# Attention of a hybrid encoder block in couples of steps instead of single steps, with the PSUM banks laid out anew

## The chip, the cores and the metric

The kernel runs on one core of one Trainium2 chip. The metric is the device time of one execution in microseconds (us); lower is better. Five engines work side by side on a core: TensorE (PE), VectorE (DVE), ScalarE (ACT), GpSimd (POOL) and SyncE (SP, which only issues DMAs here). They are kept in order by semaphores alone.

## What is computed

One layer of an encoder on 1024 tokens of width 1024, all in f32. The part that the change touches is attention over a token's own chunk of 64 and the 8 chunks before it, for 8 heads of width 64:

```
u = layer_norm(x) * (1 + sc_m) + sh_m
z_q, z_k, z_v, z_gate = pieces of u @ w_in
s = einsum('bnqhd,bnkhd->bnhqk', q, kb) + bias      # q scaled by 64 ** -0.5
p = softmax(s, axis=-1)                             # over 9 chunks, those ahead of the start left out
o = einsum('bnhqk,bnkhd->bnqhd', p, vb)
merged = gate0 * y_pool + gate1 * (o @ w_br_attn) + gate2 * y_conv
```

Around it stand adaLN conditioning, a pooling branch, a convolution branch, an output projection and an MLP. Each product is made of three fp32r products (high by high, high by low, low by high), which keeps nearly f32 accuracy; so each operand is split into a rounded part and its rest.

## The kernel before, in words

The program writes out by hand, engine by engine, in which order each instruction stands; nothing schedules it. The heads are taken in 4 pairs, each pair in 16 steps: `step_of` (L433) makes of a step number a pair, a head h of the two, and a block t of 128 queries out of 8. There are 64 steps. A step of block t has min(t+1, 5) key blocks of 128, so t = 0 to 3 are narrow and t = 4 to 7 wide (5 blocks, 640 keys).

What one step goes through:

- **scores** (PE, L2387): 2 matmuls where the keys fit one bank, else 4 (320 columns each).
- **add_scores** (DVE, L1683): the bias is added, the row's maximum taken and the result negated, in one instruction that writes `probs`, and a short one that reads the maximum out. It signals `biased`.
- **the exponential** (ACT, L1123), with the row's sum; then the sum's reciprocal (DVE, L1718); then the scaling of `probs` (ACT, a `copy`, L938). They signal `exp_done`, `inv_done` and `probs_done`.
- **transpose_probs** (PE, L2397): one 128x128 transpose per key block, into PSUM.
- **take_pt_hi** (ACT, L938) rounds the transposed weights into `pt`, **take_pt_lo** (DVE, L1701) makes the rest. `pt` has two places, for even and odd steps.
- **weigh** (PE, L2412): one matmul of 256 columns per key block, values by weights, into PSUM (`o_bank`).
- **take_low** (ACT, L938) copies one part of the result to `mid`; **add_o** (DVE, L1693 and L1695) adds the two others, one after the other, each of 64 partitions by 128 columns. It signals `o_added`, two counts a step.

The queries, keys and values of the next pair are projected meanwhile: 144 matmuls of 512 columns a pair (`project`, L2347), nine a step. In the pair's first two steps PE also transposes the values (`transpose_v`, L2368; `take_v`, `take_v_lo` take them off). `take_half` on ACT and `take_half_lo` on DVE take the projections off; `cut_hi_after` and `cut_lo_after` split the next weights.

On PE step a stands as: scores of a, five projections, transposes of a-1, four projections, weighing of a-2. On DVE (the loop after L1703): add_scores of a, what there is to take of a projection, the reciprocal of a, add_o of a-3, take_pt_lo of a-1. PSUM's eight banks of 512 f32 columns: 0 and 1 projections, 2 and 3 weighed values of even and odd steps, 4 and 5 scores (5 also transposed values), 6 and 7 transposed weights.

Of the kernel before, what the change touches and what calls it, by code (L numbers as in the profile page):

```python
# [7 lines left out]
P = 128  # L8
# [48 lines left out]
PER_STEP = PROJ // STEPS  # L57
# [16 lines left out]
def trunk_layer(nc, x, c, w_ada, b_ada, w_in, b_gate, w_pool, pool_scale, rel_bias, conv_w, conv_b,  # L74
# [180 lines left out]
    with ExitStack() as ctx:  # L255
# [189 lines left out]
        def score_cols(t):  # L445

            if width_of(t) <= HALF:
                return ps[:, 4, 0:width_of(t)]
            return ps[:, 4:6, 0:KEYS // 2]
# [16 lines left out]
        def o_bank(b, rows, part):  # L466
            return ps[rows, 2 + b % 2, part * P:(part + 1) * P]
# [291 lines left out]
        def _(pool):  # L759
# [151 lines left out]
            for t in range(4, ST - 1):  # L911
# [3 lines left out]
        HALF_STEP = {2: (0, 0), 3: (0, 1), 5: (1, 0), 6: (1, 1), 8: (2, 0), 9: (2, 1), 10: (3, 0), 11: (3, 1),  # L915
                     13: (4, 0), 15: (5, 0)}
        CUT_STEP = {7: 1, 12: 3, STEPS + 1: 5}

        def half_of(a):

            pair, i = divmod(a, STEPS)
            if 0 <= pair < PAIRS and i in HALF_STEP and not (pair == PAIRS - 1 and i in (3, 6, 9, 11)):
                return pair + 1, *HALF_STEP[i]
            return None

        def cut_of(a):

            for pair in range(PAIRS):
                if a - STEPS * pair in CUT_STEP:
                    return pair + 1, CUT_STEP[a - STEPS * pair]  # L930
            return None

        N_STEPS = PAIRS * STEPS

        @block.scalar
        def _(act):
# [137 lines left out]
            def take_v(pair, half):  # L1074
# [7 lines left out]
                if pair >= 2:  # L1082
                    act.wait_ge(pv_done, STEPS * (pair - 1))
                copy(v_high(pair % 2, slice(4 * half, 4 * half + 4)),
                     ps[:, 5, :].rearrange("p (t c d) -> p t c d", t=4, d=HEAD_DIM)).then_inc(vt_hi, 1)
# [21 lines left out]
            def take_pt_hi(b):  # L1107

                nb = blocks_of(step_of(b)[2])
                act.wait_ge(pt_done, b + 1)  # L1110
                if b >= 2:
                    act.wait_ge(pv_done, b - 1)
                copy(pt[:, b % 2, 0:nb, 0, :], banks(6)[:, 0:nb * P].rearrange("p (b q) -> p b q", q=P))\
                    .then_inc(pt_hi_done, 1)

            for a in range(N_STEPS + 3):
                pair, h, t = step_of(a)
                if a >= 3:
                    take_low(a - 3)
                if a < N_STEPS:  # L1120
                    col, w = a % STAT_COLS, width_of(t)
                    act.wait_ge(biased, a + 1)
                    nc.scalar.activation(probs[a % 2][:, 0:w], probs[a % 2][:, 0:w], ACT.Exp,  # L1123
                                         bias=neg_max[:, col:col + 1], scale=-1.0,
                                         accum_out=row_sum[:, col:col + 1]).then_inc(exp_done, 1)
                if 1 <= a <= N_STEPS:
                    take_pt_hi(a - 1)
# [1584 lines left out]
```

## Time and profile before

| what | us |
|---|---|
| median of 3 runs (1402.46 to 1402.83) | 1402.79 |
| the profiled execution, its own time | 1402.69 |
| its span (first to last instruction) | 1400.9 |
| PE busy in the span | 1380.7 (99%) |
| DVE, ACT, POOL busy | 982.4, 652.7, 429.3 |
| attention steps, from the first scores to the last weighing | about 139 to 372 |

The span is what the trace covers; the execution's own time is 1.8 us longer. Busy time of PE counts the overlapping matmuls once. A row of the timeline gives the start in us from the span's start, the duration in us, the engine and the line, what is written and read, and how many like instructions stand together; behind it, in brackets, idle time of the engine before it and what ended that. PEld is the load of the stationary operand, which runs beside the matmul before.

### The profile page before, as it was taken

Reading aid. Unit: us, or ns where it says so; the run is one execution under the profiler, and the core shown is the slowest. Engines: PE = TensorE matmul, PEld = TensorE weight load, DVE = VectorE, ACT = ScalarE, POOL = GpSimd, SP = SyncE. Lnnn points to the kernel's source line nnn. Section 1 sums busy time; section 2 is a strip of 40 time slices with the busy share of each in tenths; the row PEclk is TensorE's granted clock in tenths of the full one; section 3 lists DMA queues with packets and bytes.
Section 4 is the critical chain, followed back from the end, with each engine's and each line's share of the span. In section 5 each row is a group of like instructions: output and inputs, shape, how many; then the busy total and the mean of one; then the engine's idle time right before and its main releaser. Section 6 shows DMA issues by size and latency. Waiting matters only on the chain.

```text
span 1400.9 us, 17410 instructions
## 1 busy us (share of the span) xinstructions
PE 1380.7 (99%) x6560; PEld 1151.1 (82%) x6560; DVE 982.4 (70%) x1356; ACT 652.7 (47%) x925; POOL 429.3 (31%) x454
## 2 busy tenths in 40 slices
PE   6999999999999999999999999999999999999997
PEld 4888888888888888888888888888888888888886
DVE  7899777776499935564588797655656736447688
ACT  7523777877522133112436754444334635343251
POOL 1023655656565000000035236334344200001225
PEclk9999999999999999999999999999999999999999
DMA  9985466474665234653702645443446978466371
GB/s 344 330 277 151 137 188 172 155 198 152 205 193 173 91 105 131 219 161 120 262 8 114 217 144 195 158 156 131 150 158 224 310 265 286 171 224 239 102 228 77
DMA packets 159083, 256.42 MB, mean 183 GB/s; under 512 B 11352, under 2 KB 81422, under 8 KB 159000
## 3 DMA queue, kind: packets, MB, share of 16 engines
q1 hardware_dynamic: 144152, 204.97, 44.0%
q0 software_dynamic: 14848, 50.34, 10.8%
q8 instruction: 52, 0.85, 0.3%
q14 instruction: 31, 0.25, 0.1%
HBM read 182.36 MB, written 68.71 MB: 179 GB/s over the span
## 4 chain that ended last, share of the span: by engine, by line
PE 90%; DVE 5%; ACT 2%; SPq 1%; issue 1%; DMA 1%; DVEq 0%; ACTq 0%
PE ps L2181 23%; PE ps L2182 23%; PE ps L2183 23%; PE ps L2347 12%; PE ps L2387 2%; PE ps L2412 2%; PE ps L2397 2%; DVE bn L1426 1%; DVE mid L1877 1%; DMA ada<-in_w_ada_dram 1%; PE ps L2288 1%; PE ps L2282 1%; PE ps L2283 1%; DVE mix_tmp L1870 1%; ACT mix_tmp L961 1%
## 5 line engine op out<-in xcount | busy, mean ns | idle before, releaser
L2001 DVE TENSOR_TENSOR part_lo<-k_raw,part_hi 128x1024 fp32r<-128x1024 f32 x112 | 147.1, 1343 | 56.8 <-ACT part_hi L938 53.8
L2182 PE MATMUL ps<-part_lo,part_hi 128*128 128x512 f32 (+1 forms) x460 | 176.4, 383 | 0.0
L2183 PE MATMUL ps<-part_hi,part_lo 128*128 128x512 f32 (+1 forms) x460 | 176.4, 383 | 0.0
L2181 PE MATMUL ps<-part_hi 128*128 128x512 f32 (+1 forms) x460 | 176.4, 383 | 0.0
L2181 PE MATMUL ps<-act_hi,w_hi 128*128 128x512 f32 (+1 forms) x448 | 171.6, 383 | 0.0
L2183 PE MATMUL ps<-act_hi,w_lo 128*128 128x512 f32 (+1 forms) x448 | 170.9, 382 | 0.0
L2182 PE MATMUL ps<-act_lo,w_hi 128*128 128x512 f32 (+1 forms) x448 | 170.9, 382 | 0.0
L938 ACT ACTIVATE part_hi<-k_raw 128x1024 fp32r<-128x1024 f32 x112 | 116.4, 1059 | 111.8 <-DMA k_raw<-tw_scratch 50.2
L1420 DVE TENSOR_TENSOR w_lo<-w_raw,w_hi 128x1024 fp32r<-128x1024 f32 x51 | 67.3, 1320 | 54.6 <-ACT w_hi L938 54.6
L2181 PEld LDWEIGHTS ps<-part_hi 128*128 128x128 f32 x460 | 86.4, 188 | 17.2
L2183 PEld LDWEIGHTS ps<-part_hi,part_lo 128*128 128x128 f32 x460 | 86.4, 188 | 17.0
L2182 PEld LDWEIGHTS ps<-part_lo,part_hi 128*128 128x128 f32 x460 | 86.4, 188 | 16.9
L1343 ACT ACTIVATE h_buf<-h_buf,cols 128x1024 f32<-128x1024 f32 x28 | 32.3, 1152 | 145.6 <-DVE h_buf L1996 145.6
L2347 PE MATMUL ps<-act_hi,w_lo 128*128 128x512 f32 x240 | 99.8, 416 | 0.0
L2183 PEld LDWEIGHTS ps<-act_hi,w_lo 128*128 128x128 f32 x448 | 84.2, 188 | 16.4
L2181 PEld LDWEIGHTS ps<-act_hi,w_hi 128*128 128x128 f32 x448 | 84.2, 188 | 16.3 <-issue 0.2
L2182 PEld LDWEIGHTS ps<-act_lo,w_hi 128*128 128x128 f32 x448 | 84.3, 188 | 16.1 <-issue 0.2
L2347 PE MATMUL ps<-act_hi,w_hi 128*128 128x512 f32 x240 | 94.8, 395 | 0.0
L2347 PE MATMUL ps<-act_lo,w_hi 128*128 128x512 f32 x240 | 94.3, 393 | 0.0
L938 ACT ACTIVATE w_hi<-w_raw 128x1024 fp32r<-128x1024 f32 x52 | 54.8, 1053 | 80.1 <-PE ps L2183 74.6
L897 POOL TENSOR_TENSOR resid<-resid,q 128x512 f32<-128x512 f32 x16 | 25.3, 1609 | 218.1 <-DVE q L2062 218.1
L2181 PE MATMUL ps<-act_hi,set_hi 128*128 128x512 f32 x224 | 87.1, 389 | 0.0
(294 smaller groups left out, 3279.2 us busy)
## 6 DMA issues: line engine op xcount, KB each, us to landing
k_raw<-h_scratch SPq DMA_DIRECT2D x112, 256.0 KB, 4.5
w_raw<-in_w_in_dram SPq DMA_DIRECT2D x41, 512.0 KB, 4.1
ada<-in_w_ada_dram SPq DMA_DIRECT2D x8, 2048.0 KB, 10.9
tw_rows<-in_w_ff_dram POOLq DMA_DIRECT2D x64, 256.0 KB, 4.1
tw_scratch<-tw_sum POOLq DMA_DIRECT2D x32, 512.0 KB, 3.5
h_scratch<-h_sum POOLq DMA_DIRECT2D x64, 256.0 KB, 2.9
k_raw<-tw_scratch SPq DMA_DIRECT2D x64, 256.0 KB, 5.4
pair_raw<-in_w_ff_dram SPq DMA_DIRECT2D x13, 1024.0 KB, 6.3
```

The source lines that it names most:

```text
L897: nc.gpsimd.tensor_tensor(row, row, quad[:, t % 4, :], ALU.add).then_inc(quad_added, 1)
L938: return nc.scalar.activation(out, in_, ACT.Copy, **kw)
L1343: nc.scalar.activation(row, row, ACT.Relu, bias=cols[:, R_FF1 + n:R_FF1 + n + 1]).then_inc(relu_done, 1)
L1420: nc.vector.tensor_tensor(lo[:, :, :], raw_part(n)[:, :, :], f(hi[:, :, :]), ALU.subtract)\
L2001: nc.vector.tensor_tensor(part_lo[s][:, :, :], k_raw[rs][:, :, :], f(part_hi[s][:, :, :]), ALU.subtract)\
L2181: nc.tensor.matmul(out, sh, mh, start=first, stop=False)
L2182: nc.tensor.matmul(out, sh, ml, start=False, stop=False)
L2183: return nc.tensor.matmul(out, sl, mh, start=False, stop=last)
L2347: ins = nc.tensor.matmul(ps[:, hz % 2, :], s, v, start=kk == 0, stop=kk == 23)
L2387: ins = nc.tensor.matmul(ps[:, 4 + part, 0:n], qs[s][:, h, t * P:(t + 1) * P], kd[s][:, term, h, ks], start=term == 0, stop=term == 1)
L2397: ins = nc.tensor.transpose(banks(6)[:, cs], probs[b % 2][:, cs], ident[:, :])
L2412: ins = nc.tensor.matmul(ps[:, 2 + b % 2, 0:2 * P], vs[s][:, t + 1 - nb + m, h * P:(h + 1) * P], pt[:, b % 2, m, :, :], start=m == 0, stop ...
```

## The change

The loop over steps becomes a loop over couples of steps: COUPLES = 32, PER_PAIR = 8. Couple u holds the steps a = 2u and a+1. On PE it stands as: both weighings of couple u-2, both groups of transposes of couple u-1, scores of a, six projections, scores of a+1, twelve projections. At the first couple of a pair (i = 0) the scores of a and the six projections stand ahead of the transposes. `transpose_v` stands behind the transposes in the first two couples of a pair.

PSUM is laid out so that both steps of a couple fit: bank 2 holds the weighed values of both steps, side by side; scores take banks 3 and 4; transposed weights take the 1280 columns from bank 5 on, 640 for each step of a couple. Since engines now would meet in one bank, the readers wait for the whole couple: `take_low`, `take_pt_hi` and `take_pt_lo` wait for `couple_end(b)`, and PE waits at a couple's first weighing and first transposes until the couple before has been taken off.

The core of the diff:

```diff
         def o_bank(b, rows, part):
-            return ps[rows, 2 + b % 2, part * P:(part + 1) * P]
+            first = (2 * (b % 2) + part) * P
+            return ps[rows, 2, first:first + P]
...
+        HALF_ROUNDED = ({4: (2, 0)}, {1: (0, 0), 3: (1, 1), 4: (2, 1), 5: (3, 0)},
+                        {1: (0, 1), 2: (1, 0), 5: (3, 1), 6: (4, 0), 7: (5, 0)})
+        HALF_RESTS = ({2: (0, 1), 3: (1, 0), 4: (2, 0), 6: (3, 1)}, {1: (0, 0), 3: (1, 1), 4: (2, 1), 5: (3, 0)})
...
+        def couple_end(b):
+            return b // 2 * 2 + 2
+
+        def probs_t(b, n):
+            first = 5 * HALF + b % 2 * KEYS
+            return ps[:, :, :].rearrange("p b n -> p (b n)")[:, first:first + n]
...
             def take_low(b):
-                act.wait_ge(pv_done, b + 1)
+                act.wait_ge(pv_done, couple_end(b))
...
             def take_pt_hi(b):
-                act.wait_ge(pt_done, b + 1)
+                act.wait_ge(pt_done, couple_end(b))
                 if b >= 2:
                     act.wait_ge(pv_done, b - 1)
...
+            for u in range(COUPLES + 2):
+                a = 2 * u
+                pair, i = divmod(u, PER_PAIR)
+                if u >= 2:
+                    take_low(a - 4)
                     take_low(a - 3)
+                if 1 <= u <= COUPLES:
+                    take_pt_hi(a - 2)
                     take_pt_hi(a - 1)
+                if u < COUPLES:
+                    exponentials(a)
+                    if i == 1:
+                        take_v(pair, 1)
+                    if half_at(u, HALF_ROUNDED[0]):
+                        take_half(*half_at(u, HALF_ROUNDED[0]))
+                    scale_probs(a)
+                    exponentials(a + 1)
+                    if half_at(u, HALF_ROUNDED[1]):
+                        take_half(*half_at(u, HALF_ROUNDED[1]))
+                    if i == 6:
+                        cut_hi_after(pair + 1, 3)
+                    scale_probs(a + 1)
+                    if i == 0:
+                        take_v(pair, 0)
...
             def take_pt_lo(b):
-                dve.wait_ge(pt_hi_done, b + 1)
+                dve.wait_ge(pt_hi_done, couple_end(b))
...
+            for u in range(COUPLES + 2):
+                a = 2 * u
+                pair, i = divmod(u, PER_PAIR)
+                if u < COUPLES:
                     add_scores(a)
...
+                if 1 <= u <= COUPLES:
+                    take_pt_lo(a - 2)
+                    take_pt_lo(a - 1)
+                if u < COUPLES:
+                    invert_sum(a)
+                    add_scores(a + 1)
+                    if half_at(u, HALF_RESTS[0]):
+                        take_half_lo(*half_at(u, HALF_RESTS[0]))
+                    if i == 1:
+                        take_v_lo(pair, 1)
+                    invert_sum(a + 1)
+                    if i == 0:
+                        take_v_lo(pair, 0)
+                if u >= 2:
+                    add_o(a - 4)
                     add_o(a - 3)
+                if half_at(u, HALF_RESTS[1]):
+                    take_half_lo(*half_at(u, HALF_RESTS[1]))
...
             def transpose_probs(b):
                 pe.wait_ge(probs_done, b + 1)
-                if b >= 1:
+                if b >= 2 and b % 2 == 0:
                     pe.wait_ge(pt_lo_done, b)
...
             def weigh(b):
-                if b >= 2:
-                    pe.wait_ge(o_added, 2 * (b - 1))
-                else:
-                    pe.wait_ge(zp_done, 2)
+                if b >= 2 and b % 2 == 0:
+                    pe.wait_ge(o_added, 2 * b)
...
+            for u in range(COUPLES):
+                a = 2 * u
+                pair, i = divmod(u, PER_PAIR)
+                if u >= 2:
+                    weigh_couple(u - 2)
+                if i == 0:
                     scores(a)
+                    run(u, 0)
+                if u >= 1:
+                    transpose_probs(a - 2)
                     transpose_probs(a - 1)
+                if i < 2:
+                    transpose_v(pair, i)
+                if i > 0:
+                    scores(a)
+                    run(u, 0)
+                scores(a + 1)
+                run(u, 1)
+                run(u, 2)
```

`run(u, n)` is six projections. The arithmetic, the count of matmuls and all DMAs stay as they were; SP and POOL have the same instructions in the same order.

How the order moves on PE, in the middle of a pair. Before, a wide step from its last projection on (`probs` are the weights to be transposed, `kd` and `qs` keys and queries, `pt` and `vs` transposed weights and values):

```order
L2347 MATMUL ps<-act_hi,w_lo_57 128x512
L2412 MATMUL ps<-pt,vs_86 128x256 [waits o_added,pt_lo_done]
L2412 MATMUL ps<-pt,vs_86 128x256 x4
L2387 MATMUL ps<-kd_84,qs_82 128x320 [waits biased]
L2387 MATMUL ps<-kd_84,qs_82 128x320 x3
L2347 MATMUL ps<-act_hi,w_hi_55 128x512
L2347 MATMUL ps<-act_lo,w_hi_55 128x512
L2347 MATMUL ps<-act_hi,w_lo_57 128x512
L2347 MATMUL ps<-act_hi,w_hi_55 128x512
L2347 MATMUL ps<-act_lo,w_hi_55 128x512
L2397 MATMUL ps<-ident,probs_89 128x128 [waits pt_lo_done,probs_done]
L2397 MATMUL ps<-ident,probs_89 128x128 x4
```

Now, the head of a couple whose own steps are t = 6 and 7 (it weighs t = 2 and 3 and transposes t = 4 and 5):

```order
L2448 MATMUL ps<-pt,vs_86 128x256 [waits o_added,pt_lo_done]
L2448 MATMUL ps<-pt,vs_86 128x256 x2
L2448 MATMUL ps<-pt,vs_86 128x256 [waits pt_lo_done]
L2448 MATMUL ps<-pt,vs_86 128x256 x3
L2435 MATMUL ps<-ident,probs_89 128x128 [waits pt_lo_done,probs_done]
L2435 MATMUL ps<-ident,probs_89 128x128 x4
L2435 MATMUL ps<-ident,probs_90 128x128 [waits probs_done]
L2435 MATMUL ps<-ident,probs_90 128x128 x4
L2425 MATMUL ps<-kd_84,qs_82 128x320 [waits biased]
L2425 MATMUL ps<-kd_84,qs_82 128x320 x3
L2382 MATMUL ps<-act_hi,w_hi_55 128x512
```

Short matmuls that stood in four places of two steps stand together at the head; six and twelve projections follow the two groups of scores. The first weighing waits for `o_added`.

On DVE, before, two wide steps:

```order
L1683 ISA probs_89,neg_max<-ps,bias_rev_87 128x640 [waits pt_done,scores_done]
L1683 ISA neg_max 128x1
L1634 SCALAR_TENSOR_TENSOR qs_81<-ps,qs_81 64x512 [waits half_hi]
L1718 RECIPROCAL inv_sum<-row_sum 128x1 [waits exp_done]
L1693 TENSOR_TENSOR mid<-ps,mid 64x128 [waits o_low_done]
L1695 TENSOR_TENSOR mid<-ps,mid 64x128 [waits o_added]
L1701 TENSOR_TENSOR pt<-ps,pt 128x5x128 [waits pt_hi_done]
L1683 ISA probs_90,neg_max<-ps,bias_rev_87 128x640 [waits pt_done,scores_done]
L1683 ISA neg_max 128x1
L1634 SCALAR_TENSOR_TENSOR qs_81<-ps,qs_81 64x512 [waits half_hi]
L1718 RECIPROCAL inv_sum<-row_sum 128x1 [waits exp_done]
```

Now, the same engine in a couple with t = 6 and 7:

```order
L1704 ISA probs_89,neg_max<-ps,bias_rev_88 128x640 [waits pt_done,scores_done]
L1704 ISA neg_max 128x1
L1722 TENSOR_TENSOR pt<-ps,pt 128x5x128 [waits pt_hi_done] x2
L1729 RECIPROCAL inv_sum<-row_sum 128x1 [waits exp_done]
L1704 ISA probs_90,neg_max<-ps,bias_rev_88 128x640 [waits pt_done,scores_done]
L1704 ISA neg_max 128x1
L1729 RECIPROCAL inv_sum<-row_sum 128x1 [waits exp_done]
L1714 TENSOR_TENSOR mid<-ps,mid 64x128 [waits o_low_done]
L1716 TENSOR_TENSOR mid<-ps,mid 64x128 [waits o_added]
L1714 TENSOR_TENSOR mid<-ps,mid 64x128 [waits o_low_done]
L1716 TENSOR_TENSOR mid<-ps,mid 64x128 [waits o_added]
```

All four adds of a couple (L1714, L1716) stand behind the reciprocal of the couple's second step.

On DVE, now, the first couple of a pair (t = 0 and 1):

```order
L1704 ISA probs_89,neg_max<-ps,bias_rev_87 128x128 [waits pt_done,bias_in0,scores_done]
L1704 ISA neg_max 128x1
L1722 TENSOR_TENSOR pt<-ps,pt 128x5x128 [waits pt_hi_done] x2
L1729 RECIPROCAL inv_sum<-row_sum 128x1 [waits exp_done]
L1704 ISA probs_90,neg_max<-ps,bias_rev_87 128x256 [waits pt_done,scores_done]
L1704 ISA neg_max 128x1
L1729 RECIPROCAL inv_sum<-row_sum 128x1 [waits exp_done]
L1667 TENSOR_TENSOR vs_85<-ps,vs_85 128x4x128 [waits vt_hi]
L1714 TENSOR_TENSOR mid<-ps,mid 64x128 [waits o_low_done]
L1716 TENSOR_TENSOR mid<-ps,mid 64x128 [waits o_added]
L1714 TENSOR_TENSOR mid<-ps,mid 64x128 [waits o_low_done]
L1716 TENSOR_TENSOR mid<-ps,mid 64x128 [waits o_added]
```

Here the rest of the transposed values (L1667) also stands ahead of the adds.

## Rows read from the trace of the kernel before

**Rows 1.** Page, part 1: busy time, share of the span, instructions.

```profile
PE 1380.7 (99%) x6560; PEld 1151.1 (82%) x6560; DVE 982.4 (70%) x1356; ACT 652.7 (47%) x925; POOL 429.3 (31%) x454
```

**Rows 2.** Windows: stretch, its us, busy us by engine, granted clock, DMA share, GB/s.

```profile
139.00:372.00 233.00, 232.86 (x1333) 200.36 (x1332) 164.66 (x430) 174.56 (x377) 136.56 (x180) 1.00 0.56 166
```

**Rows 3.** Waits, PEld, 139 to 372 us: engine line waited for, us, times, longest.

```profile
PEld ps L2397 <- ACT probs L938: 1.2, 3, 0.5
```

**Rows 4.** Timeline, PE, a wide step at 244 us.

```profile
244.31 0.75 PE L2412 MATMUL ps<-pt,vs 128*128 128x256 f32 x5
244.89 0.75 PE L2387 MATMUL ps<-kd,qs 128*128 128x320 f32 x4
245.47 0.39 PE L2347 MATMUL ps<-act_hi,w_hi 128*128 128x512 f32 x1
...
246.40 0.40 PE L2347 MATMUL ps<-act_lo,w_hi 128*128 128x512 f32 x1
246.92 0.74 PE L2397 MATMUL ps<-ident,probs 128*128 128x128 f32 x5
247.41 0.47 PE L2347 MATMUL ps<-act_hi,w_lo 128*128 128x512 f32 x1
...
248.43 0.75 PE L2412 MATMUL ps<-pt,vs 128*128 128x256 f32 x5
```

**Rows 5.** Timeline, PE, a long run of 512-column matmuls behind the attention, 42 apart.

```profile
450.17 0.39 PE L2181 MATMUL ps<-act_hi,w_hi 128*128 128x512 f32 x1
...
459.69 0.39 PE L2181 MATMUL ps<-act_hi,w_hi 128*128 128x512 f32 x1
```

**Rows 6.** Timeline, DVE, the same wide step (second head of the pair, h = 1).

```profile
245.10 0.16 DVE L1718 RECIPROCAL inv_sum<-row_sum 128x1 f32<-128x1 f32 x1 [0.99 <-ACT probs L1123]
245.29 0.29 DVE L1693 TENSOR_TENSOR mid<-ps,mid 64x128 f32<-64x128 f32 x1
245.62 0.29 DVE L1695 TENSOR_TENSOR mid<-ps,mid 64x128 f32<-64x128 f32 x1
245.95 0.82 DVE L1701 TENSOR_TENSOR pt<-ps,pt 128x640 fp32r<-128x640 f32 x1
246.69 0.81 DVE L1683 CUSTOM_DVE_ANT_0 probs<-ps,bias_rev 128x640 f32<-128x640 f32 x1
247.43 0.08 DVE L1683 DVE_READ_ACCUMULATOR2_ANT neg_max<- 128x1 f32 x1
```

**Rows 7.** Timeline, DVE, a step that adds a result of the first head (h = 0).

```profile
227.34 0.16 DVE L1718 RECIPROCAL inv_sum<-row_sum 128x1 f32<-128x1 f32 x1
227.42 0.27 DVE L1693 TENSOR_TENSOR mid<-ps,mid 64x128 f32<-64x128 f32 x1
227.72 0.28 DVE L1695 TENSOR_TENSOR mid<-ps,mid 64x128 f32<-64x128 f32 x1
```

**Rows 8.** Timeline, ACT, the wide step of rows 6.

```profile
244.88 0.19 ACT L1123 ACTIVATION_READ_ACCUMULATOR probs<-probs,neg_max 128x1 f32 x1
244.97 0.69 ACT L938 ACTIVATE pt<-ps 128x640 fp32r<-128x640 f32 x1
...
247.55 0.83 ACT L1123 ACTIVATE probs<-probs,neg_max 128x640 f32<-128x640 f32 x1 [0.87 <-DVE neg_max L1683]
```

**Rows 9.** Timeline, ACT, the narrow step t = 1 of the first pair.

```profile
145.07 0.51 ACT L1123 ACTIVATE probs<-probs,neg_max 128x256 f32<-128x256 f32 x1 [2.23 <-DVE neg_max L1683]
...
146.32 0.58 ACT L938 ACTIVATE vs<-ps 128x512 fp32r<-128x512 f32 x1
```

**Rows 10.** Timeline, DVE, the same narrow step.

```profile
144.61 0.42 DVE L1683 CUSTOM_DVE_ANT_0 probs<-ps,bias_rev 128x256 f32<-128x256 f32 x1
...
146.93 0.69 DVE L1646 TENSOR_TENSOR vs<-ps,vs 128x512 fp32r<-128x512 f32 x1 [0.77 <-ACT vs L938]
```

**Rows 11.** Windows behind the last matmul; columns as in rows 2.

```profile
1393.50:1397.50 4.00, 0.09 (x1) 0.00 (x0) 3.70 (x9) 0.20 (x1) 1.44 (x1) 1.00 0.61 247
1397.50:1401.00 3.50, 0.00 (x0) 0.00 (x0) 1.03 (x3) 0.00 (x0) 0.00 (x0) 0.50 0.42 150
```

More of the change, by code:

```diff
@@ L912, in _, with half_at @@
                 add_bias(t)
[L915 to L923, printed above, removed]
-            return None
[L926 to L933, printed above, removed]
+        N_STEPS = PAIRS * STEPS
+        COUPLES = N_STEPS // 2
+        PER_PAIR = STEPS // 2
+        HALF_ROUNDED = ({4: (2, 0)}, {1: (0, 0), 3: (1, 1), 4: (2, 1), 5: (3, 0)},
+                        {1: (0, 1), 2: (1, 0), 5: (3, 1), 6: (4, 0), 7: (5, 0)})
+        HALF_RESTS = ({2: (0, 1), 3: (1, 0), 4: (2, 0), 6: (3, 1)}, {1: (0, 0), 3: (1, 1), 4: (2, 1), 5: (3, 0)})
+        def half_at(u, table):
+            pair, i = divmod(u, PER_PAIR)
+            if u < COUPLES and i in table and not (pair == PAIRS - 1 and table[i][1] == 1):
+                return pair + 1, *table[i]
+            return None
+        def couple_end(b):
[3 more added lines that the diff above has]
+            return ps[:, :, :].rearrange("p b n -> p (b n)")[:, first:first + n]
         @block.scalar
@@ L2396, in transpose_probs @@
                     cs = slice(m * P, (m + 1) * P)
-                    ins = nc.tensor.transpose(banks(6)[:, cs], probs[b % 2][:, cs], ident[:, :])
+                    ins = nc.tensor.transpose(probs_t(b, KEYS)[:, cs], probs[b % 2][:, cs], ident[:, :])
                 ins.then_inc(pt_done, 1)
@@ L2463, in _, with run, weigh_couple @@
-            for a in range(N_STEPS + 2):
-                pair, h, t = step_of(a)
-                if a < N_STEPS:
+            def run(u, n):
+                pair, i = divmod(u, PER_PAIR)
+                per = PROJ // PER_PAIR // 3
+                for m in range((3 * i + n) * per, (3 * i + n + 1) * per):
+                    project(pair + 1, m)
+            def weigh_couple(u):
+                weigh(2 * u)
+                weigh(2 * u + 1)
+            for u in range(COUPLES):
+                a = 2 * u
+                pair, i = divmod(u, PER_PAIR)
+                if u >= 2:
+                    weigh_couple(u - 2)
+                if i == 0:
@@ new lines, in _ @@
+                if i > 0:
[4 more added lines that the diff above has]
+                run(u, 2)
+            weigh_couple(COUPLES - 2)
+            transpose_probs(N_STEPS - 2)
+            transpose_probs(N_STEPS - 1)
+            pe.wait_ge(w_lo_done, N_G + 1)
+            for h in range(2):
+                pe.wait_ge(h_free[h], 3 * (PAIRS + 1))
+                ins = gate_half(N_G, 0, h)
+                if h == 0:
+                    weigh_couple(COUPLES - 1)
```

115 lines of the change are left out of this document (41 added, 74 removed).

## The prediction

> **What bounds the kernel now.** I read the page's busy times first: PE is busy 99% of the span, every other engine far less [rows 1]. So a change of order on PE is worth what it saves PE or costs it in waits. The window table of the attention steps says the same of the stretch that is changed: 232.86 of 233 us busy at the full granted clock [rows 2]. The waits of the weight loads are the third view: the largest in those 233 us is 1.2 us in three places [rows 3]. Today nobody keeps PE waiting, because each result has most of two steps to come back. The change alters who must be back when, so I then read the timelines of PE, DVE and ACT in one wide step for durations and for the time from an end to the start that it releases [rows 4, 6, 8].
>
> **Prices from the rows.** PE: five weighings take 0.58 us (244.31 to 244.89), four wide scores 0.58 (to 245.47), five transposes 0.49 (246.92 to 247.41) and somewhat more, since the matmul behind them starts late: the four projections to 248.43 take 1.02 [rows 4] where four in a long run take 0.91 (42 take 9.52 us, 0.227 each) [rows 5]. So ten transposes are 1.1, ten weighings 1.17. Six projections in a run take about 1.38, twelve 2.75. A result lands with the end of PE's row, 0.3 us after the last matmul's start: the last of the four scores starts 0.14 before 245.47, and its group's row ends at 245.64 [rows 4].
>
> DVE: a wide add_scores ends 0.82 us after its start (246.69 to 247.51, with the reading of the maximum); the exponential starts 0.04 later, at 247.55 [rows 6, 8]. A take_pt_lo holds DVE 0.74. An add of the second head (h = 1) starts 0.33 after the one before, and the reciprocal is 0.19 ahead of the first [rows 6]; with h = 0 these are 0.30 and 0.08 [rows 7], and from one step's second add to the next instruction I take 0.20 (0.28 less the 0.08 by which DVE overlaps independent instructions). So reciprocal to the end of four adds: 0.08 + 0.30 + 0.20 + 0.30 + 0.28 = 1.16 us for h = 0, 0.19 + 3 x 0.33 + 0.29 = 1.47 for h = 1. ACT: the exponential with its sum ends 0.93 after its start (0.83 less an overlap of 0.09, and 0.19 for the read); take_pt_hi holds ACT 0.6 [rows 8]. From a release by DVE to PE's matmul: the transposes at 246.92 waited for the take_pt_lo that ended at 246.77, so 0.15 [rows 4, 6].
>
> **Part 1, fewer changes between short and long matmuls.** Before, two steps have four runs of projections, now two. The run of four above costs 0.11 over the long rate, but the last transpose ahead of it shows less than its 0.11, so most of this is no cost; the run of five from 245.47 to 246.40 shows 0.93 for four intervals, 0.02 over [rows 4, 5]. I take 0.025 us a run: 2 x 0.025 x 32 = 1.6 us saved. Bounds: nothing, and 0.11 a run, 7 us.
>
> **Part 2, the small waits of today go**: 0.5 us saved, of at most 1.2 [rows 3]; the one at 246.92 cost 0.29 (0.52 from 246.40 where 0.23 is the pace) [rows 4].
>
> **Part 3, the new wait.** A couple's first weighing waits for all adds of the couple before it in the weighing order (one bank holds both steps' values), and on DVE those four adds stand behind the reciprocal of a+1. So between the scores of a+1 and the next head lies a chain, and PE has only the run of twelve, 2.75 us, to cover it. What is queued behind the weighing is everything on PE: transposes, scores, projections; all other engines wait for these in turn.
>
> *A couple with t = 6, 7* (now, first DVE listing), in us from its head. PE: 7 weighings 0.82, 10 transposes to 1.92, scores of a to 2.50, six projections to 3.88, scores of a+1 to 4.46, twelve to 7.21. DVE: scores of a are there at 2.70, add_scores holds it to 3.44; two take_pt_lo (ready: ACT had both take_pt_hi done at 3.4) to 4.93; reciprocal, 5.01; add_scores of a+1 ends 5.83; exponential 5.87 to 6.80; reciprocal from 6.84, four adds end 8.00 (h = 0) or 8.31 (h = 1); weighing 8.15 or 8.46. PE waits 0.94 or 1.25 us.
>
> *t = 4, 5*: PE has only 3 weighings and 7 transposes, twelve end at 6.40; scores of a+1 are back at 3.86, then 0.82, 0.97, 1.2 and 0.15: 7.0. Wait 0.6 or 0.9 (part of it may show at the first projection of a bank, which ACT and DVE take off late). *t = 2, 3*, the same way: 0.4 or 0.7. *t = 0, 1 in mid-pair*: 0.93, since two wide take_pt_lo stand ahead of narrow scores that PE finishes early.
>
> *t = 0, 1 at a pair's head* (last listing). PE: weighings 1.17, scores 1.39, six to 2.77, transposes to 3.87, four transposes of values to 4.31, scores 4.54, twelve to 7.29. The transposes land at 4.1; ACT's two take_pt_hi end 5.4; DVE's two take_pt_lo last to 6.87, reciprocal 6.95; the narrow add_scores takes 0.42 and ends 7.4 [rows 10]; its exponential takes 0.6 (0.51, less the overlap, and the read), 8.0 [rows 9]; reciprocal 8.2; ACT scales (0.4) and only then takes the values, 0.58 to 9.2 [rows 9]; DVE's rest of the values takes 0.69 to 9.9 [rows 10]; only then four adds with h = 1, to 11.2. Weighing at 11.4: PE waits 4.1 us.
>
> Adds are in couples 2 to 31. Sum: t = 6,7: 4 x 0.94 + 4 x 1.25 = 8.8. t = 4,5: 4 x 0.6 + 4 x 0.9 = 6.0. t = 2,3: 4 x 0.4 + 3 x 0.7 = 3.7. t = 0,1 in mid-pair: 4 x 0.93 = 3.7. Pair heads after the first: 3 x 4.1 = 12.3. Together 34.5 us in 30 places. Bounds: a chain of some nine links may be 0.25 shorter or longer a head (overlaps and releases of 0.04 and 0.08), 30 x 0.25 = 7.5 us either way.
>
> What follows the attention stays PE-bound and is only moved: DMAs and POOL have the same order and get later, not earlier. Behind the last couple 24 projections of the gate stand before and behind its weighing; I cost that at nothing, covered by those matmuls; without the cover it would be one chain, some 1 us.
>
> **The clock at the pair heads.** Behind the last matmul PE stands idle; the granted clock stays 1.00 through 1397.5 us, some 4 us, and is 0.50 in the last 3.5 us, which is the lower level, 1.2 GHz [rows 11]. A wait of 4.1 us is near that. The Trainium skill (TensorE: Matmul & The Clock Gate, section "HAM oscillation — how this bites in real kernels") warns that a longer idle gap in a matmul loop throttles the array to half rate, and that the matmuls after it are slow until activity lifts it. By that rule the sum would be some us higher, by rows 11 it is not, as the idle stretch is just about the one that was still at full clock. I keep it out of the sum and in the rivals.
>
> **Sum.** 1402.7 (the profiled execution, 0.1 us under the median) - 1.6 - 0.5 + 34.5 = 1435.1 us, 2.3% slower.
>
> **The rivals.**
>
> *The clock falls at the pair heads.* For: waits of 4.1 us, as above. Against: three places only, and at the end the fall came about 4 us after the last matmul, not earlier. Price: work of the next couple at half clock. If about 2.5 us of full-rate work is run at half rate, each fall adds 2.5, three add 7.5: 1442.6. Bounds: nothing, and a head's short matmuls and six projections twice, 3.9 us each, 11.7.
>
> *Only the pair heads wait.* If in ordinary couples the adds came ahead of their need, because DVE and ACT are quicker into each instruction when they lag behind, then 12.3 alone remains: 1402.7 - 2.1 + 12.3 = 1412.9. Against: three of the links (add_scores, exponential, adds) alone are 0.82 + 0.93 + 1.16 = 2.9 us, over 2.75.
>
> *The run of twelve covers the wait, and the change is faster.* Mechanism: the adds' bank is free in time everywhere and only the saved changes count: 1402.7 - 2.1 = 1400.6, down to 1395 at the upper bound of 0.11 a run. It decides from the point where the chain behind the scores of a+1 is under 2.9 us; I get 3.5 at the least and 6.7 at a pair's head. The long runs are real [rows 5], the chain speaks against it.
>
> *More waits than I found*, two engines kept apart in bank 2 or 5 to 7 longer than the old layout did: 1446 to 1460.
>
> **How the numbers follow.** Forecast 0.66, clock falls 0.17, only pair heads 0.08, covered 0.03, something between these two near no change 0.02, more waits 0.04. The predicted time is 1435. The range goes from 1424 (the chain 0.25 shorter everywhere and another 3 us of part 1) to 1447 (the clock rival with its upper bound, or the chain 0.25 longer with two falls). About 0.2% is what a measurement here can tell from no change. Faster 0.03, the same 0.02, slower 0.95.
>
> **What would show it.** In the changed kernel's profile the weighings' weight loads wait for DVE's second add (L1716), about 1 us behind couples with t = 6, 7 and 0, 1, less behind the narrow ones, and about 4 us behind the first couple of pairs 1 to 3: some 34 us in 30 places. Attention lasts 265 us instead of 232; PE's busy time stays about 1380; everything behind 400 us has the lengths of before. Part 1 is wrong if the runs of twelve are not near 2.75 us. The clock rival shows as a granted clock of 0.5 behind the pair heads. I am wrong if PE's waits name another releaser (take_low, take_pt_lo, the projections' banks) for more than 5 us, or if ordinary couples have a head without a wait.

## Result, and the profile after

The changed kernel takes 1441.28 us (median of 4 runs, 1440.89 to 1441.87) against 1402.62 us before (1402.31 to 1402.83): ratio 1.0275, 95% interval 1.0262 to 1.0288, so 38.7 us or 2.75% slower. The forecast was 1435.0, its range 1424 to 1447. The profiled execution took 1440.89 us with a span of 1439.1 us.

Busy times of the kernel after (page, part 1) and, below the dots, its chain of work that ended last by engine (part 4):

```profile
PE 1392.2 (97%) x6560; PEld 1156.4 (80%) x6560; DVE 966.0 (67%) x1356; ACT 651.2 (45%) x925; POOL 408.0 (28%) x454
...
PE 82%; DVE 10%; ACT 4%; issue 2%; SPq 1%; DMA 1%; DVEq 0%; ACTq 0%
```

PE falls from 99% of the span [rows 1] to 97%, while its busy time grows by 11.5 us. So the kernel lost time in two ways: PE waits, and for some time it works more slowly. DVE, which does the same work as before, now carries a tenth of the chain that sets the end, where it carried 5%.

Where the loss lies is read from windows of the kernel after (stretch, its us, busy us of PE, PEld, DVE, ACT, POOL, granted clock, DMA share, GB/s): attention, and everything behind it.

```profile
139.00:405.00 266.00, 239.82 (x1310) 202.11 (x1309) 157.83 (x428) 172.96 (x377) 156.70 (x215) 0.97 0.56 165
410.00:1434.00 1024.00, 1021.45 (x4630) 848.77 (x4628) 679.31 (x733) 409.35 (x466) 220.16 (x174) 1.00 0.49 169
```

The same stretch behind attention in the kernel before:

```profile
372.00:1395.80 1023.80, 1021.18 (x4629) 848.47 (x4627) 691.18 (x736) 414.07 (x471) 265.92 (x213) 1.00 0.51 174
```

1021 us and 1021 us: nothing is lost behind attention. In it PE has 26 us without work, where it had 0.14 in 233 us [rows 2], and the granted clock is 0.97 in the mean, not 1.00. From the first scores to the first matmul of the pooling it is 270.6 us instead of 232.3, 38.3 more: the whole loss.

What PE waits for there (waits, 139 to 405 us; the weight loads' rows, and behind the dots the matmuls' row that names the releaser):

```profile
PEld ps L2448 <- issue: 36.0, 30, 4.2
PEld ps L2382 <- issue: 2.3, 3, 0.8
PEld ps L2382 <- DVE kd L1659: 2.1, 3, 0.7
PEld ps L2403 <- DVE vs L1667: 0.3, 1, 0.3
...
PE ps L2448 <- DVE mid L1716: 24.1, 24, 3.8
```

The weighings' loads (L2448) sit idle ahead of 30 heads, and the releaser is DVE's second add (L1716). In the kernel before no wait in this stretch was over 0.5 us [rows 3]. A load's idle time begins before PE has run out of matmuls, so PE's own loss is less than 36 us. Taken from matmul to matmul, less the pace of 0.227 us, it is 29.0 us.

An ordinary couple (t = 6 and 7), on PE:

```profile
187.89 1.07 PE L2448 MATMUL ps<-pt,vs 128*128 128x256 f32 x7
188.80 1.26 PE L2435 MATMUL ps<-ident,probs 128*128 128x128 f32 x10
189.81 0.82 PE L2425 MATMUL ps<-kd,qs 128*128 128x320 f32 x4
190.47 0.39 PE L2382 MATMUL ps<-act_hi,w_hi 128*128 128x512 f32 x1
...
191.86 0.74 PE L2425 MATMUL ps<-kd,qs 128*128 128x320 f32 x4
192.44 0.39 PE L2382 MATMUL ps<-act_hi,w_hi 128*128 128x512 f32 x1
...
194.96 0.39 PE L2382 MATMUL ps<-act_hi,w_lo 128*128 128x512 f32 x1
196.28 0.95 PE L2448 MATMUL ps<-pt,vs 128*128 128x256 f32 x6 [0.93 <-DVE mid L1716]
```

and on DVE, from the second step's scores on:

```profile
192.97 0.80 DVE L1704 CUSTOM_DVE_ANT_0 probs<-ps,bias_rev 128x640 f32<-128x640 f32 x1
...
194.77 0.16 DVE L1729 RECIPROCAL inv_sum<-row_sum 128x1 f32<-128x1 f32 x1 [0.99 <-ACT probs L1120]
194.97 0.29 DVE L1714 TENSOR_TENSOR mid<-ps,mid 64x128 f32<-64x128 f32 x1
195.30 0.29 DVE L1716 TENSOR_TENSOR mid<-ps,mid 64x128 f32<-64x128 f32 x1
195.51 0.29 DVE L1714 TENSOR_TENSOR mid<-ps,mid 64x128 f32<-64x128 f32 x1
195.83 0.29 DVE L1716 TENSOR_TENSOR mid<-ps,mid 64x128 f32<-64x128 f32 x1
```

The twelve projections from 192.44 end their issue at 195.19. In that time DVE goes through add_scores, idles 0.99 us for ACT's exponential, and only then starts the adds, which end at 196.12; the weighing follows at 196.28. The adds themselves need 1.15 us, and e3 below runs them at the couple's start: it is their place in DVE's order that makes them late.

A pair's first couple, on DVE:

```profile
201.77 1.55 DVE L1722 TENSOR_TENSOR pt<-ps,pt 128x640 fp32r<-128x640 f32 x2 [1.44 <-ACT pt L939]
...
203.31 0.41 DVE L1704 CUSTOM_DVE_ANT_0 probs<-ps,bias_rev 128x256 f32<-128x256 f32 x1
...
205.62 0.69 DVE L1667 TENSOR_TENSOR vs<-ps,vs 128x512 fp32r<-128x512 f32 x1 [1.06 <-ACT vs L939]
206.34 0.29 DVE L1714 TENSOR_TENSOR mid<-ps,mid 64x128 f32<-64x128 f32 x1
```

and on PE:

```profile
203.44 0.39 PE L2382 MATMUL ps<-act_hi,w_lo 128*128 128x512 f32 x1
207.65 2.47 PE L2448 MATMUL ps<-pt,vs 128*128 128x256 f32 x10 [3.82 <-DVE mid L1716]
209.92 0.84 PE L2435 MATMUL ps<-ident,probs 128*128 128x128 f32 x3
```

The ten weighings from 207.65 to 209.92 take 2.27 us; behind a wait at full clock ten take 1.26 (those at 196.28). The windows around the three pair heads (columns as above) show why:

```profile
205.00:207.60 2.60, 0.00 (x0) 0.00 (x0) 1.78 (x5) 1.53 (x3) 1.39 (x2) 1.00 0.45 156
207.60:211.00 3.40, 3.35 (x16) 3.38 (x17) 0.00 (x0) 0.64 (x4) 2.08 (x3) 0.50 0.61 174
272.50:279.30 6.80, 5.39 (x22) 5.23 (x23) 1.91 (x9) 1.43 (x6) 3.94 (x6) 0.50 0.48 148
340.70:344.20 3.50, 3.10 (x15) 3.13 (x16) 0.26 (x1) 0.43 (x2) 2.54 (x4) 0.51 0.17 57
```

At each wait of 4 us the granted clock falls to its lower level, 1.2 GHz, for 3.4 or 6.8 us; at the second head it falls while PE still waits. PE is busy for 3.35 + 5.39 + 3.10 = 11.8 us of that. At half the pace half of it, 5.9, is lost by this estimate; e1 below measures it.

### The profile page after: what moved, and what is told of

It is laid out like the page before. It is cut to its first block, busy times and chain, and to the rows that moved or that the text cites. A ratio compares the mean times of both kernels' runs of the same rounds, so it can differ in the third digit from the quotient of the medians.

```text
span 1439.1 us, 17350 instructions
## 1 busy us (share of the span) xinstructions
PE 1392.2 (97%) x6560; PEld 1156.4 (80%) x6560; DVE 966.0 (67%) x1356; ACT 651.2 (45%) x925; POOL 408.0 (28%) x454
## 4 chain that ended last, share of the span: by engine, by line
PE 82%; DVE 10%; ACT 4%; issue 2%; SPq 1%; DMA 1%; DVEq 0%; ACTq 0%
PE ps L2216 22%; PE ps L2218 22%; PE ps L2217 22%; PE ps L2382 5%; PE ps L2448 3%; PE ps L2435 2%; PE ps L2425 1%; DVE pt L1722 1%; DVE probs L1704 1%; DVE bn L1447 1%; DVE mid L1912 1%; DVE mid L1716 1%; ACT probs L1120 1%; DMA ada<-in_w_ada_dram 1%; PE ps L2323 1%
## 5 line engine op out<-in xcount | busy, mean ns | idle before, releaser
L1441 DVE TENSOR_TENSOR w_lo<-w_raw,w_hi 128x1024 fp32r<-128x1024 f32 x51 | 62.9, 1233 | 70.6 <-ACT w_hi L939 70.3
L2382 PE MATMUL ps<-act_hi,w_lo 128*128 128x512 f32 x240 | 93.8, 391 | 0.0
```

The lines of the kernel that those rows point to most:

```text
L1441: nc.vector.tensor_tensor(lo[:, :, :], raw_part(n)[:, :, :], f(hi[:, :, :]), ALU.subtract)\
L2382: ins = nc.tensor.matmul(ps[:, hz % 2, :], s, v, start=kk == 0, stop=kk == 23)
```

## Experiments

The theory behind the first six kernels: DVE's order alone makes the waits (four adds behind the reciprocal of a+1), and the waits of 4 us bring the clock down. Rivals: the bank or the releases cost something in themselves, and the slow stretches cost nothing that one sees in the time.

**e1, no idle PE at the pair heads.** 28 matmuls of 256 columns whose result nobody reads stand ahead of the weighing at the second couple of pairs 1 to 3; DVE's chain is untouched.

```diff
+                if i == 1 and u > 1:
+                    pe.wait_ge(pt_lo_done, 2 * (u - 1))
+                    for _ in range(28):
+                        nc.tensor.matmul(ps[:, 7, PIECE:HALF], act_hi[:, 0, 0:P], act_hi[:, 0, 0:PIECE],
+                                         start=True, stop=True)
```

> The changed kernel with 28 matmuls of 256 columns into an unused half bank ahead of the weighing at the second couple of pairs 1 to 3, where PE waits about 4 us; their results are used nowhere. They take about 3.3 us of that wait and nothing waits for them. Theory A (the three falls of the granted clock to 0.50, 13.7 us of the span together, cost time of their own): the clock stays 1.00 through the attention, the wait for the adds is as long as before (about 4 us with the fill in it), and the time falls by 4 to 7 us, to about 1435 to 1437. Rival B (the slow stretches lie within what PE would have waited anyway at the next heads): clock 1.00, time unchanged at 1441.

Measured: 1435.52 us (1435.44 to 1436.25), ratio 1.0235 (1.022 to 1.025). Its pair head, on PE, and its whole attention:

```profile
205.74 1.48 PE L2497 MATMUL ps<-act_hi 128*128 128x256 f32 x11
207.69 1.43 PE L2448 MATMUL ps<-pt,vs 128*128 128x256 f32 x10 [0.48 <-DVE mid L1716]
208.97 0.49 PE L2435 MATMUL ps<-ident,probs 128*128 128x128 f32 x3
```

```profile
139.00:401.00 262.00, 245.75 (x1400) 208.49 (x1399) 158.37 (x433) 174.40 (x379) 150.67 (x204) 1.00 0.54 161
```

The head is at 207.69 as before (207.65), but the clock stays 1.00 and the ten weighings take 1.28 us, not 2.27. Doing more matmuls made the kernel 5.8 us faster: that is the price of the three falls of the clock, measured by itself, and it agrees with the estimate of 5.9.

**e2, the values' rest behind the adds.** At a pair's first couple DVE takes the rest of the transposed values (L1667) after the four adds.

```diff
                     invert_sum(a + 1)
-                    if i == 0:
-                        take_v_lo(pair, 0)
                 if u >= 2:
                     add_o(a - 4)
                     add_o(a - 3)
+                if u < COUPLES and i == 0:
+                    take_v_lo(pair, 0)
```

> The changed kernel with one DVE instruction moved: at a pair's first couple the rest of the transposed values is taken behind the four adds instead of ahead of them. Theory A (PE waits at the head for whatever stands ahead of the adds on DVE): the wait at the pair heads falls from 4.0 to about 2.3 us, three times; that is too short for a fall of the clock, which stays 1.00. 5 us of waits and 4 to 7 of clock go: 1429 to 1433. Rival B (the wait is for the weighed values' bank as such, not for the place of the adds on DVE): 1441. If the clock falls all the same: 1436.

Measured: 1433.65 us (1431.67 to 1434.95), ratio 1.022 (1.0204 to 1.0235). The first two pair heads on PE, and two windows behind the second:

```profile
205.82 1.43 PE L2448 MATMUL ps<-pt,vs 128*128 128x256 f32 x10 [2.07 <-DVE mid L1716]
...
268.73 1.52 PE L2448 MATMUL ps<-pt,vs 128*128 128x256 f32 x10 [2.09 <-DVE mid L1716]
```

```profile
268.70:269.90 1.20, 1.17 (x10) 1.20 (x11) 0.61 (x1) 0.67 (x1) 1.12 (x3) 1.00 0.10 38
269.90:273.30 3.40, 3.40 (x15) 3.21 (x14) 0.87 (x4) 1.25 (x5) 1.74 (x3) 0.50 0.38 133
```

Each pair head's wait fell from 4.0 to 2.2 us, 5.3 us together; the rest of the 7.6 us gained is clock. I had expected the clock to stay up, or else 1436; it came out between, because the first wait is followed by full clock, the second and the third (at 333.3 us) by 3.4 us at half. Both falls came only after PE had been at work again at full clock, for 1.2 and 1.5 us.

**e3, all four adds first.** They go from the end of DVE's couple to its start, ahead of add_scores of a.

```diff
+                if u >= 2:
+                    add_o(a - 4)
+                    add_o(a - 3)
                 if u < COUPLES:
                     add_scores(a)
...
                     if i == 0:
                         take_v_lo(pair, 0)
-                if u >= 2:
-                    add_o(a - 4)
-                    add_o(a - 3)
```

> The changed kernel with the four adds of a couple moved on DVE from behind the second reciprocal to ahead of the first add_scores. PSUM layout, PE's and ACT's order and all waits for whole couples stay. Theory A (the place of the adds makes the wait): no head waits for the adds, 29 us of waits go, the clock stays at 1.00; new waits of 8 to 10 us appear, since add_scores of a starts later (PE's scores of a+1 wait for it) and since values and projections are taken later: 1409 to 1413. Rival B (the shared banks and the waits for whole couples cost it, whatever the order on DVE): above 1430.

Measured: 1414.5 us (1414.26 to 1414.58), ratio 1.0084 (1.0069 to 1.0099), 1.5 us above the range I gave and far below the rival's. No weighing waits any more and the clock is 1.00 throughout attention. What loads wait for instead:

```profile
PEld ps L2428 <- DVE neg_max L1704: 7.5, 14, 1.2
PEld ps L2406 <- DVE vs L1667: 3.3, 4, 1.0
PEld ps L2385 <- issue: 2.8, 3, 0.9
PEld ps L2385 <- DVE kd L1659: 2.6, 3, 0.9
```

So 26.8 of the 38.7 us hang on where four instructions stand on DVE. The banks' layout and the bunched matmuls are as in the changed kernel, so they do not cost these 26.8 us by themselves. The shared bank still has a part in them: it is what makes a weighing wait for the adds of both steps before. The reverse, the adds at the end with a bank for each step, was not run, so it is not shown that the order alone would do the harm. But the adds now hold up add_scores, for they wait for ACT's take_low of the weighings just done (in one couple DVE idles 1.95 us for it, until 195.97), and scores, projection banks and values come late in turn.

**e4, the adds later still.** The control in the other direction: in 12 couples DVE's half of a projection (take_half_lo of the second table) stands ahead of the adds.

```diff
+                if half_at(u, HALF_RESTS[1]):
+                    take_half_lo(*half_at(u, HALF_RESTS[1]))
                 if u >= 2:
                     add_o(a - 4)
                     add_o(a - 3)
-                if half_at(u, HALF_RESTS[1]):
-                    take_half_lo(*half_at(u, HALF_RESTS[1]))
```

> The changed kernel with one more DVE instruction ahead of the adds in 12 couples: the take of a projection's rest (about 0.68 us) that stood behind them. Theory A: each of the 12 heads waits longer by 0.65 to 0.95 us (that take also waits for ACT's rounding behind the second scaling): 8 to 11 us more, 1449 to 1452. Rival B (the adds' place is not what PE waits for): 1441 to 1442.

Measured: 1457.73 us (1456.09 to 1458.88), ratio 1.0389 (1.0371 to 1.0406), above what I expected.

```profile
PEld ps L2448 <- issue: 48.5, 30, 4.2
```

```profile
213.10:216.50 3.40, 3.40 (x16) 3.40 (x17) 0.00 (x0) 0.80 (x4) 1.28 (x2) 0.50 0.66 202
```

The loads' wait grew by 12.5 us, 1 us in each of the 12 couples instead of the 0.7 of the instruction, because it waits itself for ACT's part. Five heads that had waited 0.9 us waited 2.2, and behind three of these the clock fell too: six falls instead of three. Cause and sign are as the theory has them; it was the size of the clock's part that I left out.

**e5, the adds split.** Those of the couple's first step stand first, those of the second behind add_scores of a+1.

```diff
+                if u >= 2:
+                    add_o(a - 4)
                 if u < COUPLES:
                     add_scores(a)
...
                     add_scores(a + 1)
+                if u >= 2:
+                    add_o(a - 3)
```

> The changed kernel with the adds of a couple parted on DVE: those of its first step stand ahead of the first add_scores, those of its second step right behind the second add_scores, ahead of the second reciprocal. Theory A: with only half of the adds ahead of add_scores of a, PE's scores of a+1 hardly wait, and the second half still comes before the head, for DVE has 1 us there while ACT makes the exponential. What stays are waits for the projections' banks (about 6 us), for the values (2) and at the pair heads for the adds (3 x 0.9): 1408 to 1412, a little under the kernel with all adds first (1414.5). Rival B (the couple-wise waits of the layout are what is left of the loss): no better than 1414.

Measured: 1413.02 us (1411.8 to 1413.96), ratio 1.0073 (1.0058 to 1.0089), 1.0 us above the range and below the rival's 1414. Two of its loads' waits:

```profile
PEld ps L2385 <- issue: 3.9, 3, 1.3
...
PEld ps L2451 <- issue: 3.3, 3, 1.1
```

Ordinary weighings have no wait; the pair heads still have 0.87 us each, and the projections' banks (L2385) about 1.

**e6, what was left of e5 taken away.** At a pair's first couple the second step's adds come right behind add_scores of a, and ACT takes the values right behind the first exponential; in the third and seventh couple DVE takes its half of the projection ahead of the second add_scores.

```diff
-                    if i == 1:
-                        take_v(pair, 1)
+                    if i < 2:
+                        take_v(pair, i)
...
                     scale_probs(a + 1)
-                    if i == 0:
-                        take_v(pair, 0)
...
                     add_scores(a)
+                if u >= 2 and i == 0:
+                    add_o(a - 3)
...
+                if i in (2, 6) and half_at(u, HALF_RESTS[0]):
+                    take_half_lo(*half_at(u, HALF_RESTS[0]))
                 if u < COUPLES:
                     add_scores(a + 1)
+                if u >= 2 and i != 0:
+                    add_o(a - 3)
```

> The kernel of the last row with three more moves: at a pair's first couple all four adds stand ahead of the transposed weights' rest, the values are taken right behind the first exponential on ACT and behind the second reciprocal but with nothing more behind them on DVE, and the two takes of a projection's rest that came just too late (couples 2 and 6 of a pair) stand ahead of the second add_scores. PE's order and the layout are those of the change. Theory A (the change lost its time to the order on DVE and ACT alone; the saved changes between short and long matmuls are real): waits of PE in the attention fall to about 2 us, and the time is 1399 to 1404, between 3 us under and 1.5 us over the kernel before. Rival B (the layout with its couple-wise waits costs of itself): 1406 or more.

Measured: 1404.49 us (1404.2 to 1405.03) against 1402.62 before, ratio 1.0012 (1.0003 to 1.002): 0.5 us above the top of my range, and under the 1406 that the rival asked for. So 36.8 of the 38.7 us came back with PE's order and the banks as changed; only the readers' order differs. Its loads' waits in attention:

```profile
PEld ps L2430 <- DVE neg_max L1702: 2.3, 6, 0.6
PEld ps L2440 <- ACT probs L939: 2.1, 6, 0.4
```

**e7, e8 and e9, those waits too.** In e7 ACT's cut of the weights at the seventh couple goes behind the scaling of the second step.

```diff
-                    if i == 6:
-                        cut_hi_after(pair + 1, 3)
                     scale_probs(a + 1)
+                    if i == 6:
+                        cut_hi_after(pair + 1, 3)
```

> The kernel of e6 with ACT's cut of the weights at the seventh couple of a pair moved behind the scaling of the couple's second step. In e6 the second group of transposes of the next couple waits 0.35 us for that scaling in three places. If what is left of e6 against the kernel before is waits alone, three times 0.35 goes: 1404.5 - 1.05 = 1403.4 us (1403.1 to 1403.8), and DVE's rounding of the same weights, which comes some 0.8 us later, costs nothing because the adds behind it have until the next couple's head. Rival: the later rounding delays DVE's next add_scores, and PE waits for scores' banks or transposes elsewhere by as much: 1404.2 to 1404.8.

In e8, besides, the rest of the second step's transposed weights goes behind the second add_scores at a pair's first couple.

```diff
                     take_pt_lo(a - 2)
-                    take_pt_lo(a - 1)
+                    if i != 0 or u == COUPLES:
+                        take_pt_lo(a - 1)
...
                     add_scores(a + 1)
+                if i == 0 and 1 <= u < COUPLES:
+                    take_pt_lo(a - 1)
```

> As e7, and at a pair's first couple DVE takes the rest of the second step's transposed weights (take_pt_lo of a-1) only behind add_scores of a+1. In e6 the transposes at the second couple's head wait 0.21 us in three places, because both wide take_pt_lo stand ahead of the narrow add_scores. If waits alone are left, 3 x 0.21 more goes: 1402.8 us (1402.4 to 1403.3), which is the kernel before, and no more than 0.5 us is left of visible waits; then the couples' longer runs bring under 1 us by themselves. Rival: fewer changes between short and long matmuls are worth the 1.6 us that I gave them, and the two kernels come out 1 us or more below the kernel before: under 1401.6.

Measured: e7 1406.56 us (1406.32 to 1406.88), e8 1405.17 us (1404.3 to 1406.01). Both lie above their ranges, by 2.8 and by 1.9 us. In e7 its rival came true, and more. DVE in e7, at the eighth couple:

```profile
186.28 1.23 DVE L1439 TENSOR_TENSOR w_lo<-w_raw,w_hi 128x1024 fp32r<-128x1024 f32 x1 [1.84 <-ACT w_hi L939]
...
188.19 0.82 DVE L1702 CUSTOM_DVE_ANT_0 probs<-ps,bias_rev 128x640 f32<-128x640 f32 x1
```

The cut saved 0.35 us on PE in three places, but DVE's rounding of the same weights stands in line behind it, so add_scores starts 1.3 us after its scores have landed and the next scores wait about 1 us for their bank. In e8 the transposes wait no more, and it is 1.4 us faster than e7, but the waits for the scores' bank stay (0.97, 0.97 and 1.45 us in the three places). e9 moves the rounding to the end of the next couple:

```diff
-                elif u < COUPLES and i in (4, 6):
-                    cut_lo_after(pair + 1, i - 3)
+                elif u < COUPLES and i in (4, 7):
+                    cut_lo_after(pair + 1, 1 if i == 4 else 3)
```

> As e8, and DVE's rounding of the weights at the seventh couple of a pair (1.23 us) moved behind the last work of the eighth. In e7 and e8 that rounding waits 1.8 us for ACT's cut, and the add_scores behind it comes so late that PE waits 0.97 us (once 1.45) for the scores' bank in three places. If these waits are all that is left of e8 (visible sum 3.9 us with 0.4 and 0.2 elsewhere), 3.4 goes: 1405.2 - 3.4 = 1401.8 us (1401.3 to 1402.4), level with the kernel before or under it by under 0.1%. Rival: the rounding only meets the next pair's first couple, where DVE has two wide take_pt_lo and four adds: waits of about 1 us there, 1404 to 1405.5.

Measured: 1404.0 us (1403.02 to 1404.41) against 1402.72, ratio 1.0008 (0.9999 to 1.0017): level with the kernel before. That is 1.6 us above the top of my range and at the lower edge of the rival's, but not by the rival's mechanism: half of the wait that I expected to go stayed in its old place, 0.5 us in each of three, and at the next pair's first couple PE waits 0.3 us, once. The sum of these visible waits is 2.3 us in e6 and 2.2 in e9, while attention up to the pooling lasts 233.70 and 233.29 us against 232.30 before. Without them it would be about 1 us shorter than before. That is a difference and not a run of its own, but it is all that these runs leave for the bunching.

**e10, one rounding too late.** The rounding at the fifth couple goes to the end of the sixth.

```diff
-                elif u < COUPLES and i in (4, 7):
-                    cut_lo_after(pair + 1, 1 if i == 4 else 3)
+                elif u < COUPLES and i in (5, 7):
+                    cut_lo_after(pair + 1, 1 if i == 5 else 3)
```

> As e9, and the rounding at the fifth couple of a pair moved to the end of the sixth. In e8 one place behind it waits 0.38 us. If only waits count, up to 0.4 less than e9: 1401.4 us (1400.9 to 1402.2). Rival: the same length as e9 or 1 us above it, since the rounding now stands ahead of the seventh couple's first add. In neither case under 1400.6 unless the longer runs of projections bring over 1 us by themselves.

Measured: 1424.92 us (1423.59 to 1427.05), far outside.

```profile
PEld ps L2390 <- DVE w_lo L1439: 17.4, 5, 4.4
```

Those weights are wanted in the sixth couple itself, so projections waited 4.1 us in three places and 3.5 in a fourth, each with a fall of the clock. I had read who stands behind the rounding on DVE, not who waits for its result.

No version was found that is faster than the kernel before.

## Why the prediction was right

*What bounds the kernel* held: PE, so that a wait on it counts in full. Everything lost lies in attention, and the chain behind it kept its length.

*Part 3, the new wait.* The mechanism and its place are shown by e3 to e6, and its size was right nearly link by link. For t = 6, 7 and h = 1 I had the weighing 8.46 us after the couple's head, 1.25 of it waiting; it came after 8.39 (187.89 to 196.28), 1.09 of it waiting. With h = 0 it was 0.90 for 0.94. At a pair's head I had the weighing after 11.4 us and a wait of 4.1; it came after 11.37 (196.28 to 207.65), 4.0 of it waiting. The mid-pair couples with t = 0, 1 waited 0.88 for 0.93, those with t = 2, 3 0.38 and 0.56 for 0.4 and 0.7. The one place where my number for the head was off is t = 4, 5 in pairs 0 to 2: 0.12 and 0.22, not 0.6 and 0.9. In the last pair, where no projections' bank holds PE up, the same heads waited 0.60 and 0.78. In pairs 0 to 2 the rest of the wait went where the prediction had a bracket, to a projections' bank:

```profile
185.43 0.69 DVE L1659 TENSOR_TENSOR kd<-ps,kd 64x512 fp32r<-64x512 f32 x1
```

```profile
186.18 0.50 PE L2382 MATMUL ps<-act_hi,w_hi 128*128 128x512 f32 x1 [0.27 <-DVE kd L1659]
```

PE loses 0.43 to 0.52 us there, in six places, while DVE's chain runs on. It makes 2.8 us, and with the heads' 29.0 it is 31.8. To this comes a price that was in none of my steps. The first weighing after a wait takes 0.19 us to the next instead of 0.117: seven weighings from 187.89 to 188.80 take 0.91, not 0.82. That is 2.3 us in 30 places (the intervals from one weighing to the next sum to 27.0 us in e1 and 24.7 in e3, both without clock falls). Together 34.1 us, against 34.5 in the sum; that this agrees so well is luck, for two errors of over 2 us cancelled.

*The clock at the pair heads* is the step that failed. I kept it out of the sum, and so put it at nothing, because the clock had stayed up for some 4 us behind the last matmul [rows 11]; one case is no bound, and the wait was as long as that stretch. The granted clock fell to 0.50 at all three heads. e1 gives its price as 5.8 us, where the rival had 7.5 and the sum none. It is nearly the whole difference of 6.2 us between 1435.1 and 1441.3. The Trainium skill (TensorE: Matmul & The Clock Gate, section "HAM oscillation — how this bites in real kernels") says that an idle gap in a matmul loop brings half rate behind it. I had set the row against that, and the traces of the three heads agree with the page. In e2 two of three waits of 2.2 us, half as long, had a fall behind them too.

*Parts 1 and 2.* 34.1 + 5.8 = 39.9 us of cost against 38.7 measured leaves 1.2 saved, where I had 2.1; e6 and e9 give about 1. If part 2's 0.5 us is in it, part 1 was worth some 0.7 and not 1.6. A change between short and long matmuls is nearly free: the interval from the last transpose at 247.39 to the projection is 0.03 us and the next 0.31, together 0.34, which is also what the paces of the two, 0.11 and 0.23, add up to. The bound of 7 us was far off. Twelve projections take 2.75 us (192.44 to 195.19), as predicted.

*What would show it.* Attention up to the last weighing lasts 265.0 us, as I wrote, but by luck: 24 projections of the gate, 5.6 us, now stand behind that weighing and had stood before it, so the stage I summed was 270.6. PE's busy time did not stay at 1380: it grew by 11.5 us, of which the slow stretches explain half. Waits with another releaser came to 4.7 us of idle loads, under the 5 that I had set as a limit.

What stays open: why two waits of one length can differ in what the clock does after them, whether the order on DVE as changed would have lost anything with the old banks, and whether a layout exists in which e9's last 2.2 us of waits go without making others.

## What to carry to other kernels

When work on the bounding engine is bunched, write down for each reader engine what stands ahead of the instruction that frees the shared buffer: here four instructions of 1.15 us in all stood behind a reciprocal that waits for another engine. Moving them alone gave back 26.8 of 38.7 us (e3), and with a few more moves on DVE and ACT it was 36.8 (e6). A wait of some us on TensorE has to be priced with the slow stretch behind it, and filling the wait with matmuls that nobody reads removes that part. Before an instruction is moved later on its engine, look at both who is queued behind it (e7) and who waits for its result (e10).

## What the runs showed of the hardware that was not expected

- In attention the granted clock fell at waits well under 4 us. Each wait of 3.5 to 4.1 us had a fall in it or behind it (three in the changed kernel, three in e4, four in e10). Of eight waits between 2.16 and 2.25 us (three in e2, five in e4) five had one and three had not; waits of 1.84 us and less had none. In the records it was always 0.50 or 1.00, and a fall lasted 3.4 or 6.8 us.
- A fall also came without such a wait. In the profiles of e2, e6, e8 and e9 the clock was at its lower level for 3.4 us from about 31 us on, 108 us ahead of attention, where TensorE had waited no longer than 0.6 us since 14 us and was issuing small matmuls, some of one column. The other eight profiles have the same order there and no fall. In e6:

```profile
31.40:34.80 3.40, 3.40 (x10) 2.45 (x9) 3.15 (x6) 3.37 (x5) 0.00 (x0) 0.50 1.06 373
```

- The fall need not begin with the wait. In the changed kernel's first pair head the clock was 1.00 for the idle stretch up to 207.60 us and 0.50 from the restart on, so no idle time was at the lower clock and all of it fell on the work behind. At its second head it fell 1.4 us before the restart, at the second head of e2 1.2 us after it.
- Behind a wait, the first weighing of a group took 0.08 us longer to the next one than the others did, at full clock (0.19 us, not 0.117).
- Two adds of different steps start 0.21 us apart on DVE (195.30 to 195.51), two of one step, the second of which adds to the result of the first, 0.33 (194.97 to 195.30).
